# Four of the last sixteen vector adds move to GpSimd

## The reference

```python
y = jnp.concatenate([oa, ob], axis=-1) @ w_out[l]
x = x + gate[:, None, :] * rms_norm_2(y, g_post[l])
```

## Time and profile before

| | us |
|---|---|
| median of 3 runs | 2175.1 |
| lowest and highest | 2171.84 and 2181.6 |
| the profiled execution | 2179.99 |
| its span, first to last instruction | 2178.2 |
| mean granted TensorE clock | 0.975 of full speed |

### The profile page before, as it was taken

One profiled execution on the slowest core, in us unless ns is written; L12 is line 12 of the kernel. 1 busy time (PEld: TensorE's weight loads), 2 busy tenths in 40 slices (PEclk: granted clock), 3 DMA queues, 4 the chain that ended last, 5 costly groups with the idle time before them and its releaser, 6 DMA issues.

```text
span 2178.2 us, 23708 instructions
## 1 busy us (share of the span) xinstructions
PE 2053.9 (94%) x9228; PEld 1596.7 (73%) x9228; DVE 1110.3 (51%) x1536; ACT 871.5 (40%) x1315; POOL 57.2 (3%) x111
## 2 busy tenths in 40 slices
PE   4899999999888899999999999999999999999795
PEld 1678876656777778888888888887787777776474
DVE  5685747555665555533354333436434444436534
ACT  4443345555443332222243222335324663446432
POOL 0001100000000000000000000000010000000000
PEclk8999999999999999999999999999999999999898
DMA  8235410000204546523333333334331000003042
GB/s 329 94 112 201 155 39 10 17 33 1 88 1 145 174 146 194 183 97 124 121 102 136 97 97 103 125 121 145 100 116 45 32 29 29 20 20 126 22 162 97
DMA packets 62686, 217.12 MB, mean 100 GB/s; under 512 B 6640, under 2 KB 7792, under 8 KB 62320
## 3 DMA queue, kind: packets, MB, share of 16 engines
q1 hardware_dynamic: 49008, 163.17, 22.3%
q0 software_dynamic: 13568, 52.43, 7.0%
HBM read 187.79 MB, written 25.17 MB: 98 GB/s over the span
## 4 chain that ended last, share of the span: by engine, by line
PE 82%; DVE 7%; ACT 4%; DMA 3%; issue 3%; SPq 1%; DVEq 0%; ACTq 0%
PE ps L902 20%; PE ps L904 20%; PE ps L903 20%; PE ps L1036 8%; DMA w_raw<-in_weights 3%; PE ps L1012 2%; PE ps L1013 2%; PE ps L979 2%; ACT w_hi L1251 1%; PE ps L994 1%; DVE w_lo L1645 1%; DVE slot L1641 1%; PE ps L982 1%; SPq L2187 1%; DVE x1c L1963 1%
## 5 line engine op out<-in xcount | busy, mean ns | idle before, releaser
L902 PE MATMUL ps<-h_hi,w_hi 128*128 128x512 f32 x1504 | 600.9, 400 | 34.7 <-DVE h_lo L1678 15.0
L904 PE MATMUL ps<-h_hi,w_lo 128*128 128x512 f32 x1504 | 590.0, 392 | 0.0
L903 PE MATMUL ps<-h_lo,w_hi 128*128 128x512 f32 x1504 | 589.9, 392 | 0.0
L1645 DVE TENSOR_TENSOR w_lo<-w_raw,w_hi 128x1024 fp32r<-128x1024 f32 x222 | 271.9, 1225 | 517.0 <-ACT w_hi L1251 515.8
L1251 ACT ACTIVATE w_hi<-w_raw 128x1024 fp32r<-128x1024 f32 x222 | 234.8, 1058 | 549.3 <-DMA w_raw<-in_weights 547.5
L902 PEld LDWEIGHTS ps<-h_hi,w_hi 128*128 128x128 f32 x1504 | 285.8, 190 | 100.6 <-issue 26.3
L904 PEld LDWEIGHTS ps<-h_hi,w_lo 128*128 128x128 f32 x1504 | 284.8, 189 | 60.9
L903 PEld LDWEIGHTS ps<-h_lo,w_hi 128*128 128x128 f32 x1504 | 285.3, 190 | 58.9 <-issue 1.9
L1769 DVE TENSOR_REDUCE mh<-ps 128x1 f32<-128x512 f32 x192 | 124.8, 654 | 150.6 <-PE ps L979 70.5
L902 PE MATMUL ps<-hid_hi,w_hi 128*128 128x512 f32 x352 | 136.9, 389 | 0.0
L903 PE MATMUL ps<-hid_lo,w_hi 128*128 128x512 f32 x352 | 136.9, 389 | 0.0
(11 more groups left out here) (297 smaller groups left out, 2604.3 us busy)
## 6 DMA issues: line engine op xcount, KB each, us to landing
w_raw<-in_weights SPq DMA_DIRECT2D x222, 512.0 KB, 3.5
ada_next<-in_ada POOLq DMA_DIRECT2D x32, 512.0 KB, 4.6
ada_last<-in_ada POOLq DMA_DIRECT2D x24, 512.0 KB, 4.3
ada_first<-in_ada SPq DMA_DIRECT2D x8, 1024.0 KB, 16.6
m_scratch<-y POOLq DMA_DIRECT2D x12, 512.0 KB, 4.9
xt<-in_x SPq DMA_DIRECT2D x2, 2048.0 KB, 11.7
y<-m_scratch SPq DMA_DIRECT2D x4, 1024.0 KB, 6.0
x_again<-in_x SPq DMA_DIRECT2D x16, 256.0 KB, 3.8
```

Of the source, the lines that this page charges most:

```text
L902: e.matmul(o, w_hi[slot][:, tile_of(kw)], hi, start=start, stop=False)
L903: e.matmul(o, w_hi[slot][:, tile_of(kw)], lo, start=False, stop=False)
L904: return e.matmul(o, w_lo[slot][:, tile_of(kw)], hi, start=False, stop=stop)
L1645: return e.tensor_tensor(dst, src, hi.bitcast(F32), ALU.subtract)
```

## The change

For half 1 VectorE still multiplies all eight tiles but adds the residual only to the even ones. GpSimd has a new part of step `yt`: for n = 1 and odd k it waits for VectorE's multiplication and for the residual, adds, and raises a new semaphore `y3_late`. SyncE waits for both semaphores before it sends a pair. To keep the number of semaphores, `small_in` is dropped: the load of `small` now counts on `const_in`, and all three waits at the start are for 64 on it.

```diff
-                e.wait_ge(s["y3_n"], i)
-                e.wait_ge(s[f"xb_in{n}"], 64)
-                tt(t, t, xb[:, n, k, :], ALU.add).then_inc(s["y3_add"], 1)
+                if n == 0 or k % 2 == 0:
+                    e.wait_ge(s["y3_n"], i)
+                    e.wait_ge(s[f"xb_in{n}"], 64)
+                    tt(t, t, xb[:, n, k, :], ALU.add).then_inc(s["y3_add"], 1)
...
+            def y_add(n, k):
+                if n and k % 2:
+                    e.wait_ge(s["y3_n"], 8 * n + k + 1)
+                    e.wait_ge(s[f"xb_in{n}"], 64)
+                    e.tensor_tensor(yo[:, n, k, :], yo[:, n, k, :], xb[:, n, k, :], ALU.add).then_inc(s["y3_late"], 1)
...
-                    e.wait_ge(s["y3_add"], 8 * n + k + 1)
+                    e.wait_ge(s["y3_add"], 8 + k // 2 + 1 if n else k + 1)
+                    if n:
+                        e.wait_ge(s["y3_late"], k // 2 + 1)
...
-                e.wait_ge(s["const_in"], 48)
+                e.wait_ge(s["const_in"], 64)
...
-                    e.wait_ge(s["small_in"], 16)
+                    e.wait_ge(s["const_in"], 64)
...
-                e.dma_start(small[:, :], a["small"]).then_inc(s["small_in"], 16)
+                e.dma_start(small[:, :], a["small"]).then_inc(s["const_in"], 16)
```

More of the change, by code:

```diff
@@ L74 @@
 SEMAPHORES = (
-    "small_in const_in mask_in cond_in cond_made masks_made x_in "
+    "const_in mask_in cond_in cond_made masks_made x_in "
     "ada_in0 ada_in1 ada_in2 ada_first0 ada_first1 ada_first2 ada_first3 ada_first4 ada_first5 ada_done scale_made "
@@ L93 @@
     "y2_out fsel_in pos_in swap_in z_kept ob_kept ob_in sz_in fz_in fg_act fg_vec fg_tr cols_made cum_hi cum_lo ang sines fsel_made rope2 "
-    "gate2 mix2_hi mix2_lo post_made xb_in0 xb_in1 y3_out y3_n y3_add out0 out1 ").split()
+    "gate2 mix2_hi mix2_lo post_made xb_in0 xb_in1 y3_out y3_n y3_add y3_late out0 out1 ").split()
 class Plan:
@@ L2168, in spill @@
                 e.dma_start(ob_dram[k], y2[SQ + k][:, :]).then_inc(s["ob_kept"], 16)
-            work = {"start": start, "cond": condition, "adal": ada_load, "rtab": rope_tables, "keep": keep, "keep_x1": keep_x1,
+            def y_add(n, k):
[3 more added lines that the diff above has]
+                    e.tensor_tensor(yo[:, n, k, :], yo[:, n, k, :], xb[:, n, k, :], ALU.add).then_inc(s["y3_late"], 1)
+            work = {"yt": y_add, "start": start, "cond": condition, "adal": ada_load, "rtab": rope_tables, "keep": keep, "keep_x1": keep_x1,
                     "ft": final_normed, "y2": keep_z, "spill": spill, "set3": set3}
```

## The result

| | before | after |
|---|---|---|
| median of 6 runs | 2174.83 us | 2187.55 us |
| lowest and highest | 2171.84 and 2181.60 | 2181.26 and 2191.26 |
| the profiled execution, and its span | 2179.99, 2178.2 | 2181.26, 2179.1 |

The ratio is 1.0046 with a 95% interval of 1.0026 to 1.0066, that is 10 us slower, 5.7 to 14.4. The forecast was 2176.9 in a range of 2169 to 2184: the sign of the likeliest case was right, the size far too small, and the median lies outside the range.

A forecast was written before the change was run, and what follows sets the result against it. TensorE, busy 94% of the span, bounds the kernel; only VectorE's 10.71 us tail is in reach. With 7.81 + 4.4 + 0.27 = 12.48 us there, 1.8 later, median 2175.1 becomes 2176.9 us, range 2169 to 2184.

The forecast's parts named there:

- the likeliest case: In the tail, VectorE and GpSimd exclude each other with an add near 1.1 us: 1.8 us later, 2176.9, chance 55%.
- VectorE without four adds, 7.81 us: In the tail, VectorE's twelve remaining instructions alone take 7.81 us, so it is done 2.90 us earlier.
- GpSimd's add, 1.1 us between 0.53 and 1.92: Each of four tail adds on GpSimd: 1.1 us, twice the memset; bounds from one memset and from the casts.
- The cost of a first call: About 6 us on a freshly loaded kernel's first GpSimd call, quoted from the skill; the sum would be some 8 us later.
- Whether they run side by side: Whether GpSimd's adds overlap VectorE's tail instructions; it decides the sign. The side-by-side rival: 1.8 us less, 2173.3, chance 28%.
- the first cast: GpSimd's cast at 38.01 took 0.89 us, later ones 0.29; read as exclusion beside VectorE or a 0.60 us first-use cost.
- The sum under exclusion, 12.48: Tail: VectorE's 7.81, four GpSimd adds 4.4 and lost overlaps 0.27 give 12.48 us against 10.71, 1.77 later.
- Its 3.2 us to the end I keep: Behind the last add: the last store is issued when that add ends, and the span still ends 3.2 us later.
- GpSimd's waits have nothing queued behind them but its own adds: At the end, GpSimd's added waits hold up only its own adds; its last earlier instruction is a transfer issued at 1821.94.
- The start costs nothing: At the start, dropping `small_in` costs nothing; at most 0.3 us between two landings is at stake.
- the 16.5 that I had named as a sign of being wrong: At the start, ScalarE's first square later than 16.5 us would break the claim that the merged semaphore costs nothing.
- The bounds: The range 2169 to 2184: outer cases 2173.3 and 2180.2, widened by somewhat less than the runs' 3.3 and 6.5 us.

The follow-up runs named there:

- the PSUM run: The changed kernel, but in half 1 VectorE's eight multiplies and four adds take their second operand from PSUM; 2180.65 us, one execution.
- The semaphores alone: The kernel before with only the two start semaphores merged, all adds on VectorE; 2174.65 us against 2176.98, ratio 0.9999.
- the second series: The changed kernel again, 11 runs against 34 of the kernel before; 2183.29 us against 2176.98, ratio 1.0034 (1.0020 to 1.0047).

## Why the prediction was wrong

- *VectorE without four adds, 7.81 us.* Right: with nothing contending, in the PSUM run, VectorE was done 7.76 us after its first multiply began.
- *GpSimd's add, 1.1 us between 0.53 and 1.92.* 1.26 us, 0.16 more an add. The cost of a first call that the prediction quotes, about 6 us, doesn't show in the tail: the first add took 1.64 us as the second and third did.
- *Whether they run side by side.* They exclude each other, as the likeliest case had it, and the PSUM run shows it for these adds. What made the first cast slow stays open: it takes 0.87 to 0.90 us in all twelve traces, each time beside the same VectorE instruction, so nothing here separates the port from a first use.
- *The sum under exclusion, 12.48.* 11.97. With the true 1.26 my sum would give 13.1, so a GpSimd add doesn't cost VectorE its whole length. The round of two multiplies and an add takes 2163.18 - 2160.30 = 2.88 us, 1.93 alone: a delay of 0.95 us, and 7.81 + 3 x 0.95 + 0.04 + 1.26 = 11.96. Whether the port is held for less than the add or VectorE's own start goes on meanwhile, no run separates. The two misses, +0.64 and -1.15, partly cancel, by luck: +1.26 instead of +1.77.
- *"Its 3.2 us to the end I keep", and "GpSimd's waits have nothing queued behind them but its own adds".* This is the step that failed. GpSimd's closing drain was queued behind them. I asked what the moved instructions wait for and not what the end of the program waits for. Giving GpSimd work at the end put that drain on the path, which the prediction had at nothing: 8.16 us from the last add to the end and not 3.2, +4.9 us, four times the term I argued over. The record of it stood in the trace of before, but in none of the summary views.
- *The start costs nothing.* Right in the times: the semaphores alone give 0.9999. ScalarE's first square starts at 16.67 us in the changed kernel, 0.2 later and past the 16.5 that I had named as a sign of being wrong. The sign was drawn too tight: it starts between 16.41 and 16.67 in the nine traces with the merge, and between 16.44 and 16.51 in the three without.
- *The bounds.* The mechanisms shown add up to 6.2 us, 2181.0 over the median of before (2181.4 with the 0.35 outside the span). That is inside my range, but the first series' median was 2187.55, the second's 2183.29. My upper end took in only 3.8 of the 6.5 us of spread that I had read; with all of it the end would be 2186.7, and the first series' median still outside. The spread has a known size. VectorE's first multiply comes at 2158.5, 2159.0, 2159.2, 2160.3, 2161.2, 2164.3 and 2165.7 us in seven traces whose work ahead of it is the same but for the waits at the start, and by and large later where the mean granted clock is lower (0.980, 0.978, 0.979, 0.978, 0.977, 0.975, 0.974). What remains of 12.7 - 6.2 in the first series wasn't traced; its interval reaches down to 5.7. A rival stays untested: the executions of the changed kernel have lower mean clocks (median 0.974 and 0.976 in the two series, against 0.978 in the second series' 34 of before). The 4.9 us more at the end, where the granted clock is 0.50, lower the mean by about 0.001, an estimate from these figures; whether the rest is chance or comes of the change isn't shown.

## What to carry to other kernels

An engine that finished long ago may have a closing step that the summary views don't show; give it work at the end and that step becomes the end of the kernel. Ask of each moved instruction what its new engine still has to do behind it. And in a queue that issues both stores and loads, a store that waits for compute holds every load behind it: look at the order of that queue before moving arithmetic.

## What the runs showed of the hardware

- GpSimd's first drain after its transfers ends 7.75 to 7.93 us behind its last instruction (once in each of twelve traces), and the closing one 0.07 us behind it if such a drain ran before and only adds came in between (two traces). The closing drains of TensorE, ScalarE and VectorE end within 0.06 us (two traces).
- A GpSimd add of two 128x512 float32 tiles takes 1.26 us; beside VectorE instructions that read two SBUF tiles 1.64, and each such add delays VectorE by 0.95 us; with one VectorE operand in PSUM neither is slowed (one trace).
- Moving four 512 KB stores, which wait for VectorE, off the queue that issues the weight loads gave 10 us (6 to 14) in this kernel.
